# A two-layer hybrid backbone: modulation in plain fp32, part of the second layer's preparation moved into the first layer's expert stage, and the first layer's normalized tiles taken two per unit

## What is computed

```python
sh1, sc1, gt1, sh2, sc2, gt2 = split(silu(c) @ w_mod[l] + b_mod[l], 6)     # the same for c_ctx
hx = modulate(rms_norm(x, g_norm1[l]), sh1, sc1)                           # the same for the context
zx = hx @ w_in[l]
...   # attention, hyena(z, filter(l)), conformer, gates, w_out
x  = x + gt1 * branch_merge(zx, o_attn_x, lp)
hx2 = modulate(rms_norm(x, g_norm2[l]), sh2, sc2)
x  = x + gt2 * moe(hx2, ...)
def hyena_filter(n, lp):      # depends on the layer's weights alone
    h = sin(freq * (feat @ w1 + b1)); h = sin(freq * (h @ w2 + b2)); h = (h @ w3) * decay
    return h / sum(abs(h), axis=0)
```

## Time and profile before

| quantity | value |
|---|---|
| median of 3 runs | 1641.7 us |
| the profiled execution's own time | 1633.28 us |
| its span, first to last instruction | 1631.1 us |
| mean granted TensorE clock | 0.918 of full |
| TensorE busy | 1358.5 us (83%) |
| VectorE busy | 714.5 us (44%) |
| ScalarE busy | 490.1 us (30%) |
| bytes moved | 383.55 MB |

### The profile page before, as it was taken

The page is one execution under the profiler, slowest core; times in us unless marked ns, Lnnn a source line. Parts: engine busy times, 40 slices in busy tenths (PEclk is TensorE's granted clock), DMA queues, the critical chain, the costliest instruction groups (busy, mean ns, idle before and its releaser), DMA issues.

```text
span 1631.1 us, 19353 instructions
## 1 busy us (share of the span) xinstructions
PE 1358.5 (83%) x7726; PEld 868.9 (53%) x7726; DVE 714.5 (44%) x1120; ACT 490.1 (30%) x683; POOL 50.9 (3%) x50
## 2 busy tenths in 40 slices
PE   5889999999999459999799377989999727777893
PEld 4678777677776123333233166888788612222231
DVE  4865676665462601111111478587777341010112
ACT  4852335452341300000000068446556300000000
POOL 0000000000040010000000100000002000000000
PEclk9999999999999679999999689999999958888897
DMA  9685743211220199789989586453234069999895
GB/s 353 251 345 212 309 155 124 73 63 61 100 75 1 71 352 381 297 308 373 386 329 383 187 310 237 154 207 129 104 105 154 28 245 409 388 403 394 351 411 188
DMA packets 64333, 383.55 MB, mean 235 GB/s; under 512 B 9617, under 2 KB 14293, under 8 KB 24789
## 3 DMA queue, kind: packets, MB, share of 16 engines
q1 hardware_dynamic: 45658, 341.00, 54.3%
q10 hardware_dynamic: 14490, 24.42, 4.7%
q0 software_dynamic: 4096, 16.91, 2.9%
HBM read 360.92 MB, written 43.38 MB: 248 GB/s over the span
## 4 chain that ended last, share of the span: by engine, by line
issue 41%; PE 39%; DVE 10%; ACT 5%; POOL 2%; DMA 2%; ACTq 0%; POOLq 0%; DVEq 0%
PE bank L1390 8%; PE bank L1391 8%; PE bank L1392 8%; DVE wlo L867 3%; PE bank L1422 2%; PE bank L1423 2%; POOL m_lo L515 1%; PE bank L1368 1%; ACT whi L549 1%; PE bank L1600 1%; ACT L549 1%; DMA hrow_d<-in_hy_bias 1%; PE bank L1578 1%; PE bank L1469 1%; PE bank L1403 1%
## 5 line engine op out<-in xcount | busy, mean ns | idle before, releaser
L1677 PE MATMUL bank<-wexp,xg 128*64 128x512 f32 (+1 forms) x1504 | 298.7, 648 | 67.3 <-DMA wexp<-in_expert 64.0
L867 DVE TENSOR_TENSOR wlo<-stage,whi 128x2048 fp32r<-128x2048 f32 x104 | 240.3, 2319 | 49.8 <-ACT whi L549 48.1
L1390 PE MATMUL bank<-h_hi,whi 128*128 128x512 f32 (+1 forms) x640 | 223.9, 350 | 9.8 <-DVE h_lo L867 7.7
L549 ACT ACTIVATE whi<-stage 128x2048 fp32r<-128x2048 f32 x104 | 197.7, 1905 | 76.2 <-PE bank L1392 41.4
L1391 PE MATMUL bank<-h_lo,whi 128*128 128x512 f32 (+1 forms) x640 | 219.4, 343 | 0.0
L1392 PE MATMUL bank<-h_hi,wlo 128*128 128x512 f32 (+1 forms) x640 | 219.0, 342 | 0.0
L1677 PEld LDWEIGHTS bank<-wexp,xg 128*64 128x64 f32 (+1 forms) x1504 | 79.6, 131 | 245.5 <-issue 149.3
L549 ACT ACTIVATE yrow<-bank 128x512 f32<-128x512 f32 (+1 forms) x47 | 24.0, 511 | 442.8 <-PE bank L1692 364.5
L1692 PE MATMUL bank<-wexp,act_a 128*32 128x256 f32 (+1 forms) x1056 | 149.4, 512 | 6.1 <-DVE act_a L867 6.1
L1313 DVE COPY gu_sb<-bank 128x512 f32<-128x512 f32 x47 | 32.5, 691 | 266.1 <-PE bank L1677 266.0
L1390 PEld LDWEIGHTS bank<-h_hi,whi 128*128 128x128 f32 x640 | 123.6, 193 | 31.1 <-DVE h_lo L867 8.9
(11 more groups left out here) (249 smaller groups left out, 1675.6 us busy)
## 6 DMA issues: line engine op xcount, KB each, us to landing
wexp<-in_expert SPq DMA_DIRECT2D x192, 1024.0 KB, 15.7
stage<-in_mod SPq DMA_DIRECT2D x48, 1024.0 KB, 5.9
stage<-in_in SPq DMA_DIRECT2D x40, 1024.0 KB, 4.9
x_rows<-in_c_zero SPq DMA_DIRECT2D x21, 512.0 KB, 7.0
y_rows<-in_c_zero SPq DMA_DIRECT2D x21, 512.0 KB, 7.7
stage<-in_out SPq DMA_DIRECT2D x8, 1024.0 KB, 4.8
xpick<-x_rows ACTq DMA_DIRECT2D x30, 256.0 KB, 9.3
y_rows<-yrow ACTq DMA_DIRECT2D x56, 128.0 KB
```

The source lines that it names most:

```text
L549: return nc.scalar.activation(out_, in_, f, **kw)
L867: return V.tensor_tensor(o, x, y, op)
L1390: MM(o, w[0], x_[0], start=start, stop=False)
L1677: ins = MM(bank[0][g * w:(g + 1) * w, :], x_[:, 2 * j + k, :], wexp[:, z, j, c], start=(first_ == 0), stop=(last_ == 0))
```

## The change

- **Modulation.** No split: the product takes the unit as loaded, in plain fp32, as 8 matmuls of 256 columns with a stationary side of 32 columns (`cst` is [128, 8, 32]), four column groups in turn. `modrow` is a copy of 128 rows; `fold` sums the four groups. A modulation unit's buffer is free when its product is done.
- **Unit order.** A class `UnitOrder` gives each layer its own. Layer 0 keeps the order; only units other than `mod` are split (`parts`), `in` 0 while `mod` 14 is handled. Layer 1 has no modulation ahead of `in` 0: after each `in` j come `mod` 8+2j and 9+2j. Its input units alternate in buffers 0 and 1, its modulation units in buffers 2 and 3 (a fourth one).
- **Lead units.** `mod` 0 to 7 of layer 1 are loaded by the SP queue behind the overflow experts' weights, into buffers that are free by then, the eighth when the first product is done. Their products, copies and columns, and VectorE's `modulation(0)` for layer 1, come between the expert stage and the combination.
- **Filter of layer 1.** Its loads (1.2 MB, from ScalarE's queue) come at step 1 of layer 0's expert stage, its matmuls on TensorE at steps 3, 7, 11, 13, 17, 20 and 22, VectorE's part at steps 4 to 23, ScalarE's at 6, 10 and 16.
- **Input tiles.** Layer 0 does two per unit in `mod` 8 to 11. Layer 1 does squares, sums, root and all eight tiles in a row at its start.

```diff
     fold = np.zeros((128, 2))
-    fold[0:4] = np.concatenate([np.eye(2), np.eye(2)])
+    for g in range(4):
+        fold[32 * g:32 * g + 2] = np.eye(2)
...
-        cst = keep("cst", [P, KT, P], f32r)
+        cst = keep("cst", [P, KT, 32])
-        modrow = keep("modrow", [4, 2, UW])
+        modrow = keep("modrow", [P, 2, UW])
...
+    LEAD = 8
+        def __init__(self, mods_first, mods_each, lead):
+            units, buffer, j0 = [("mod", j) for j in range(lead, mods_first)], [], mods_first
+            for j in range(8):
+                units += [("in", j)] + [("mod", j0 + mods_each * j + i) for i in range(mods_each)]
+            self.lead, self.mods = lead, 24 - lead
...
+                self.first_tile.append(self.total)
+                self.total += self.tiles[kind]
+            self.parts = [n for n in range(self.count) if units[n][0] != "mod"]
+            self.part = {n: p for p, n in enumerate(self.parts)}
+            self.ahead = {n: [] for n in range(self.count)}
+            if lead == 0:
+                self.ahead[self.at["in", 0] - 2].append(0)
+            for j in range(8):
+                self.ahead[self.at["in", j]].append(j + 1)
+            self.ahead[self.first_gate - 1].append(9)
+            for n in range(self.first_gate, self.count - 2):
+                self.ahead[n].append(self.part[n] + 2)
+            self.issue = list(range(self.count))
+            self.buffer = [n % RING for n in range(self.count)]
+            if lead:
+                self.issue = [self.at["in", 0], self.at["in", 1]]
+                for j in range(8):
+                    self.issue += [self.at["mod", j0 + mods_each * j + i] for i in range(mods_each)]
+                    if j < 6:
+                        self.issue.append(self.at["in", j + 2])
+                self.issue += range(self.first_gate, self.count)
+                for n, (kind, j) in enumerate(units):
+                    if kind == "in":
+                        self.buffer[n] = j % 2
+                    elif kind == "mod":
+                        self.buffer[n] = 2 + j % 2
+                    else:
+                        self.buffer[n] = (n - self.first_gate) % RING
...
+    orders = [UnitOrder(16, 1, 0)] + [UnitOrder(LEAD, 2, LEAD) for l in range(1, DEPTH)]
...
+        H = at_byte("H", [P, 2, 2, SEQ], f32, CONV)
...
+        raw = stage + [at_byte("raw3", [P, UE], f32, R9)]
+        lead_at = [R6, R4, R4 + 8 * K] + [R1 - 48 * K + 8 * K * i for i in range(3)] + [R3, R6]
+        lead = [at_byte(f"lead{j}", [P, UE], f32, off) for j, off in enumerate(lead_at)]
...
                 def unit(l, n):
-                    if n >= RING:
-                        sp.wait_ge(sem(l, "hi"), n - RING + 1)
-                        sp.wait_ge(sem(l, "lo"), n - RING + 1)
-                    sp.dma_start(stage[n % RING][:, :], unit_source(l, n)).then_inc(sem("all", f"w{n % RING}"), 16)
+                    o, before_ = orders[l], orders[l].previous[n]
+                    if before_ is not None and before_ in o.part:
+                        sp.wait_ge(sem(l, "hi"), o.part[before_] + 1)
+                        sp.wait_ge(sem(l, "lo"), o.part[before_] + 1)
+                    elif before_ is not None:
+                        sp.wait_ge(sem(l, "zr"), o.tiles_to(before_))
+                    sp.dma_start(raw[o.buffer[n]][:, :], unit_source(l, n)).then_inc(sem("all", landed(l, n)[0]), 16)
                 T = span(l)
...
+                    def lead_unit(j):
+                        sp.dma_start(lead[j][:, :], A["mod"][l + 1, j]).then_inc(S("lead_a" if j < LEAD // 2 else "lead_b"), 16)
+                    sp.wait_ge(S("h2"), seqs(l) * KT)
+                    lead_unit(0)
+                    sp.wait_ge(S("H_ok"), 2)
+                    lead_unit(1)
+                    lead_unit(2)
+                    for i in range(3):
+                        sp.wait_ge(S(f"used0{3 + i}"), plan.uses[0])
+                        lead_unit(3 + i)
+                    assert len(plan.steps) % XR >= 2
+                    sp.wait_ge(S("xT_mm"), len(plan.steps))
+                    lead_unit(6)
+                    for i in range(RING):
+                        sp.wait_ge(S(f"used0{i}"), plan.uses[0])
+                        unit(l + 1, orders[l + 1].issue[i])
+                    sp.wait_ge(S("zr"), total + 1)
+                    lead_unit(7)
                 sp.sem_inc(sem("all", "engine_done"), 1)
...
+                    fn(h_hi[:, k, :], hm[:, k % 2, :], ACT.Copy).then_inc(S("h_hi"), 1)
+                if l > 0:
+                    for k in range(KT):
+                        input_square(k)
+                    split(0)
+                    input_root()
+                    for k in range(KT):
+                        input_tile(k)
...
-                def split(n):
-                    act.wait_ge(sem("all", f"w{n % RING}"), 16 * (l * len(range(n % RING, NU, RING)) + n // RING + 1))
-                    if n >= RING:
-                        act.wait_ge(S("zr"), first_tile[n - RING + 1])
-                    fn(whi[n % RING][:, :], stage[n % RING][:, :], ACT.Copy).then_inc(S("hi"), 1)
+                def split(p):
+                    name, value = landed(l, parts[p])
+                    act.wait_ge(sem("all", name), value)
+                    if p >= RING:
+                        act.wait_ge(S("zr"), order.tiles_to(parts[p - RING]))
+                    fn(whi[p % RING][:, :], raw[order.buffer[parts[p]]][:, :], ACT.Copy).then_inc(S("hi"), 1)
                 def tile_ready(m):
...
+                        for k in range(2):
+                            input_tile(2 * (n - H_SLOT) + k)
...
+                aside = l < DEPTH - 1
                 for s in range(STEPS):
+                    if aside and s == 1:
+                        filter_loads(act, l + 1)
+                        load(l, "fil_in", decay_n[:, :, :], A["c_decay"])
+                        load(l, "fil_in", fwd_n[:, :, :, :], A["c_fwd"])
+                    if aside and s in (6, 10):
+                        sine(2 + (s - 6) // 4)
+                    if aside and s == 16:
+                        for t in range(2):
+                            magnitude(2 + t, hfil_n, habs_n)
...
+                if l < DEPTH - 1:
+                    for j in range(LEAD):
+                        m = total + j
+                        act.wait_ge(S("zr"), m + 1)
+                        if j >= 2:
+                            act.wait_ge(S("modcol"), order.mods + j - 1)
+                        fn(modrow[:, j % 2, :], bank[4 + j % 2][:, 0:UW], ACT.Copy).then_inc(S(f"zf{m % 2}"), 1)
                 act.sem_inc(sem("all", "engine_done"), 1)
                 if l == DEPTH - 1:
...
                 dve.wait_ge(S("y_out"), (count + STEPS) * 64)
                 dve.sem_inc(S("rows_ok"), 1)
+                if l < DEPTH - 1:
+                    modulation(0, order.mods + LEAD, l + 1)
                 for t in range(NT + 1):
...
-                def mod_columns(jj):
-                    mm = first_tile[at["mod", jj]]
+                def mod_product(o, w):
+                    for k in range(KT):
+                        g = 32 * (k % 4)
+                        ins = MM(o[g:g + 32, 0:UW], cst[:, k, :], w[:, k, :], start=(k < 4), stop=(k >= 4))
+                    return ins
...
+                def input_sums(k0, k1):
+                    for k in range(k0, k1):
+                        pe.wait_ge(S("n1_sq"), k + 1)
+                        MM(bank[2][:, :], ones[:, :], sq1[:, k, :], start=(k == 0), stop=(k == KT - 1)).then_inc(S("n1_stat"), 1)
+                if l > 0:
+                    input_sums(0, KT)
...
-                        for k in range(KT):
-                            MM(bank[m % 2][:, 0:UW], cst[:, k, :], hi[:, k, :], start=(k == 0), stop=False)
-                            ins = MM(bank[m % 2][:, 0:UW], cst[:, k, :], lo[:, k, :], start=False, stop=(k == KT - 1))
-                        ins.then_inc(S("zr"), 1)
+                            pe.wait_ge(sem("all", "c_silu"), 1)
+                        mod_product(bank[m % 2], unit_view(l, raw[order.buffer[n]], n)).then_inc(S("zr"), 1)
...
+                def filter_step(s):
+                    if s in (3, 7):
+                        i = (s - 3) // 4
+                        if i == 0:
+                            pe.wait_ge(S("fil_in"), 16 * 12)
+                        else:
+                            pe.wait_ge(S("f_sin"), 3)
+                        filter_hidden(i, l + 1, bank[6][0:64, 0:SEQ])
+                    if s in (11, 13):
+                        t = (s - 11) // 2
+                        if t == 0:
+                            pe.wait_ge(S("f_sin"), 4)
+                        else:
+                            pe.wait_ge(S("f_raw"), 3)
+                        filter_taps(t, bank[6])
+                    if s == 17:
+                        pe.wait_ge(S("f_abs"), 4)
+                        filter_total(habs_n)
```

(23 more changed lines are left out.)

400 lines of the change are left out of this document (240 added, 160 removed).

## The result

The changed kernel takes 1616.4 us (median of 4, 1614.69 to 1624.88), the kernel before 1640.6 beside it: ratio 0.9864, 95% interval 0.9824 to 0.9904. Faster by 24 us, 1.4%; 1605 (1583 to 1633) was predicted, a gain of 36.5. The profiled execution after took 1614.8 us, span 1612.6, against 1631.1: -18.5 us. The table has the stretches between the events that the prediction's terms name, in the two traces (us). Events are starts of instructions; `zraw` is ScalarE's copy of one tile of an input unit's product, so that the second `zraw` of a layer ends its `in` 0; `yrow` is its copy of expert output.

What follows compares the result with a forecast made beforehand. It took splitting and ordering to bound the barrier stretch, TensorE the input units, either TensorE or DMA the first expert stage. Terms -14-7+8+29-52.5+0=-36.5 us from the median 1641.7 gave 1605, range 1583 to 1633.

Steps and rivals of the forecast that it cites:

- the trade of the gap for the barrier stretch: Between the layers +29 us, waiting for the eighth lead unit; layer 1 from barrier to `in` 0's second tile -52.5 us.
- The gathers are late as well, but not last: Between the layers: gathers of expert rows, interleaved with lead units, land late, but the eighth lead unit ends last, at 940.4.
- two of the signs that were to show the prediction wrong: Lead units landing before the gathers do; TensorE waiting for modulation loads in layer 1.
- The product's price: Each modulation product, eight matmuls in four column groups: 0.97 us on TensorE, or 3.4 to 4.0 if nothing overlaps.
- Pairs: Layer 0's eight pairs: each 1.1 us shorter by the cheaper product, less some waits; -7 us, ends -10 and +3.
- layer 0 ahead of `in` 0: Layer 0 up to its first input unit: earlier sums and tiles, then a late load; -14 us, ends -6 and -18.
- The expert stage: Layer 0's expert stage: 3.1 us for filter tables plus 0.6 and 4.3 of unhidden matmuls; +8 us, ends +3 and +14.
- Triples: Layer 1's input units with two modulation units each: +2, -4 and +2 sum to 0 us, ends -4 and +15.
- Groups that don't overlap: Rival: column groups don't overlap, a product takes 3.4 us, the kernel is slower at 1680 us; chance 0.03.
- Slow two-buffer loads: Rival, layer 1's `mod` 8 to 23: loads taking 15 us to land would make the kernel 1673 us; chance 0.04.
- The gap was neither cheaper nor dearer: Two rivals between the layers: gap +21, about 1592 us, chance 0.16; gap +37 with waits, about 1621 us, chance 0.13.
- no other dependence filled the barrier stretch: Rival: after the barrier, tile chain or `in` 1's split halves the gain to 26 us, near 1632; chance 0.06.

Runs made afterwards that it cites:

- `groups_off`: Changed kernel with all eight matmuls of a modulation product in the same 32-column group, not four in turn; 1692.1 us, one run.
- `one_tile`: Changed kernel with layer 0 doing one tile of x per modulation unit over `mod` 8 to 15, as before; 1614.3 us, ratio 0.9891 to before.
- `filter_loads_only`: Changed kernel with layer 1's filter inputs (1.2 MB) loaded but unused and zeros in place of the spectrum; 1606.3 us, one run.

## Why the prediction was right, and where not

The direction and the range were right, the gain was not: 24 us by the medians and 18.5 between the two profiles, where 36.5 were worked out. The two largest terms hold, partly by errors that cancel; three others fall short.

**Right for the named reasons: the trade of the gap for the barrier stretch.** +29 and -52.5 were worked out, +28.4 and -51.9 measured. The first holds two errors that cancel, so that its closeness is partly luck. The eighth lead unit was there 29.8 us after the last `yrow` copy and not 35.3, and products 4 to 7 took 12.2 us and not 7.6, since all four ran at 1.2 GHz and not "a good unit of it". The sum of the bytes was right (22.1 MB at 410 GB/s from 882 to 936, for 22.3 at 402), but not which transfer came last. "The gathers are late as well, but not last" is wrong of the transfers: the fourth gather, at whose landing `comb` began in the kernel before, landed at 932.8, the eighth lead unit at 933.3, the last gather at 938.1. It is right only of what `comb` waited for, which was the products until 946.2. This row also answers two of the signs that were to show the prediction wrong: the lead units did land before the last gathers, and TensorE did wait for modulation loads in layer 1, twice, for 1.12 and 0.23 us. Neither cost much here. That "this is the price of the change" was right, but two fifths of the price are an order: 11.6 us go with one line.

**The product's price: right.** 1.07 us against 0.97, and 3.62 without groups, inside the 3.4 to 4.0 that was given. Timeline of PE, layer 1:

```profile
1006.85 0.50 PE L1606 MATMUL bank<-tables,modrow 128*128 128x2 f32 x4
1007.28 1.07 PE L1598 MATMUL bank<-stage,cst 128*32 128x256 f32 x16
```
```profile
998.69 1.07 PE L1598 MATMUL bank<-stage,cst 128*32 128x256 f32 x16
999.58 1.05 PE L1598 MATMUL bank<-raw,cst 128*32 128x256 f32 x16
```

Between the 128-column matmuls and the 32-column ones there is no gap in the rows. But the ends of matmuls are modelled in the profile, so that the missing gap, on which the prediction rested too, excludes little. From start to start a product takes 0.89 us when another product follows (998.69 to 999.58) and 1.00 us when its columns do (915.37 to 916.37 in the gap). So what the change from four groups back to the whole array costs is at most some 0.11 us, for which the sum had nothing; over the prediction's 24 products that is under 3 us. The Trainium skill (TensorEngine Tiling (Array Packing), section Key Properties) says that a change of the tiling mode drains TensorE; the 0.11 us are compatible with it, and no run here shows that a drain is what they are.

**Pairs: right**, -5.5 against -7, and -4.3 to -7.1 over the twelve profiles without `groups_off`.

**The step that was mis-sized most: layer 0 ahead of `in` 0**, -14 predicted, -4.0 measured, -2.5 to -6.6 over the ten profiles with the same start. 6.2 us of the missing 10 were gone by the first `hm`, at 59.2 and not 53. "Sums end near 35" became 39.3: TensorE waited until 24.8 for the filter's inputs, which had been there at 22.1 before the change, and its first block of sums took 5.62 us and not 3.7, in part as slow as at 1.2 GHz (the product ahead of it took 1.94 us). "Two matmuls of 0.93 us" for the magnitudes took 3.78. From the first `hm` on some 4 us more were lost. ScalarE did the eight tiles in 14 us, as worked out, but "from there ScalarE paces" was wrong for the load of `in` 0: `one_tile` took the tiles' pace away without effect, and TensorE at 1.2 GHz, 2.81 us per unit, was behind the load's issue at 73.8 instead of 66. The load landed after 6.3 us and not 4.9, and the tile behind it was 1.6 us slower than allowed. The prediction had put 1.7 us of half clock into the whole stretch; making TensorE's work smaller left it sparser and slower (granted clock 0.50 in the window of 65 to 70 us, 1.00 before the change and in `groups_off`).

**The expert stage: mechanism right, size off.** +8 predicted and +8.5 measured in that execution, but +13 in the median of eleven. The term "1.2 MB cost 3.1 us of DMA" measured 6 in one execution without the work, and 3 to 9 against the kernel before, by the fifth `yrow` copy; the 4.9 us for work that is not hidden measured 7.

**A stretch without a term: layer 1 from `mod` 23 to the experts**, 0 predicted, +6.4 measured, +2.7 to +7.8 in all. Its instructions are the same, its start is not. Timelines of DVE and ACT, before and then after:

```profile
1114.49 0.42 DVE L867 TENSOR_TENSOR hyo<-bank,zhy 128x256 f32<-128x256 f32 x1
...
1115.92 0.37 ACT L549 ACTIVATE modrow<-bank 4x256 f32<-4x256 f32 x1 [3.90 <-PE bank L1423]
```
```profile
1089.65 1.90 ACT L638 ACTIVATE whi<-stage 128x2048 fp32r<-128x2048 f32 x1
1091.45 0.38 ACT L638 ACTIVATE modrow<-bank 128x256 f32<-128x256 f32 x1
...
1091.90 2.29 DVE L1005 TENSOR_TENSOR wlo<-stage,whi 128x2048 fp32r<-128x2048 f32 x1
1094.11 0.42 DVE L1005 TENSOR_TENSOR hyo<-bank,zhy 128x256 f32<-128x256 f32 x1
```

Before, VectorE formed `hyo` ahead of the copy of `mod` 23; after, 2.7 us behind it, because ScalarE did the second gate unit's half of the split only between the last two copies. The first softmax comes 2.9 us later against that copy, and 2.6 us or more later in all the others but `groups_off` (1.2). The cause is read from the timelines and not shown: no run moved that split. For the other 3 us there is only a coincidence, the granted clock, below 0.9 in five of twenty windows of 10 us against two before; whether it is the cause, and why it falls more often, is open.

**Triples: right as a sum** (+0.7 against 0), with a wait of 4 us in the last one that nobody had priced.

**The rivals.** Groups that don't overlap would have been +77 us and were excluded by the very rows named. Slow two-buffer loads did not come: two waits, 1.12 and 0.23 us. The gap was neither cheaper nor dearer, and no other dependence filled the barrier stretch (35.1 us against 34.5). Of the missing 18 us (-18.5 against -36.5), layer 0's start is 10, the stretch behind the triples 6, the pairs 1.5.

## What to carry to other kernels

When many transfers are moved into one window, its length is set by what lies in the queue ahead of the one transfer that work waits for, and bytes that others move at the same time make each MB ahead of it dearer (here 3.7 us per MB instead of 2.5). So order the queue by who is waited for, and look at what stands behind the waiting instruction on its engine. A shorter matmul in a stretch that is not matmul-bound can be paid back partly by a lower granted clock, as ahead of `in` 0 and in the gap here: price the rest of such a stretch at 1.2 GHz as well, as one end of the range. And compare several executions before trusting a stage's length to a few us.

## What the hardware showed beside this

- With loads of 1.2 MB from a second queue, partly in small packets (`filter_loads_only`), the step that waits for weights came 6.2 us later, where a mean rate of 402 GB/s gives 3.1.
- Expert stages with the same instructions took 351.2 to 356.2 us in different executions; 3 of the 4.5 us between the quickest and the median arise at the waits of one step.
- At 1.2 GHz a product of four groups takes 1.94 us and its columns 1.02; at 2.4 GHz 1.07 and 0.61.
